# Causal mask of the attention scores added by VectorE in PSUM instead of by mask products on TensorE

## The chip, the core and the metric

The kernel runs on one NeuronCore of a Trainium2 chip (trn2). The core has TensorE for matrix products and transposes into PSUM, VectorE and ScalarE, which can read and write PSUM, GpSimd (POOL), which works on SBUF, and a queue for the DMAs on SyncE. Each engine runs its own instructions in the order in which they are written; between engines there are only semaphores. The metric is the device time of one launch in microseconds, lower is better.

## The reference

Two layers, each on 512 tokens of width 1024. In each, one normalised input goes through a combined projection to three groups of mixers: a gated delta rule (4 heads), native sparse attention (8 query heads of 64, 2 KV heads) and a short convolution. They are joined by an output projection, and a SwiGLU FFN follows. With 512 tokens there are 8 blocks of 64 and the 16 blocks that a query may choose take in all of them, and the window of 512 reaches back to the first token. So both the selected and the window branch are plain causal attention over all earlier tokens:

```
p_s = masked_softmax(jnp.einsum("bqgrd,bgqkd->bgrqk", q_r, k_g) * scale, smask)   # smask: kpos <= tq
p_w = masked_softmax(jnp.einsum("bqgrd,bkgd->bgrqk", q_r, kb) * scale, wmask)     # wmask: 0 <= dist < WINDOW
return gt[..., 0:1] * o_c + gt[..., 1:2] * o_s + gt[..., 2:3] * o_w
```

## The kernel before

The kernel writes the program of each engine as a function of the layer: `tensor_layer`, `scalar_layer`, `pool_layer`, `vector_layer`. The order of the work is written out by hand. Large products are done in three passes of fp32r (high x high, high x low, low x high), which is why weights and activations are split into a high and a low part.

A layer has three stages: the input projection with the work of the delta rule between its groups, the attention loop, and the output projection with the FFN. The change lies in the attention loop, which comes twice, once per layer.

The loop counts slots k from 0 to 23 (`N_SLOTS`), with some tail slots. `slot_of(k)` gives a pair of heads p (one of each KV head, a = 0 and 1), a branch br (selected or window) and a step s. Step 0 holds the query tiles 0 and 1, step 1 tile 2, step 2 tile 3 (`tiles_of`). The scores of one slot lie in two PSUM banks, one per a, and slots take turns between banks 0/1 and 2/3. For s = 0 tile 0 lies in columns 0 to 255 and tile 1 in 256 to 511; for s = 1 and 2 the tile has 384 or 512 columns. The causal mask matters only in the diagonal block of 128 columns of each tile, and in tile 0 for columns 128 to 255, which are computed only because products are 256 wide.

What each engine does in slot k, in its order:

- TensorE: `scores(k)`, which waits for the exponentials of slot k - 2 (line 1077), makes 6 products per tile (line 1083) and then adds the mask as products of a bf16 identity with the mask table `negm` (lines 1093, 1096). The last of them raises the semaphore `score`. Then come `p_transpose(k - 3)` (line 1109), which waits for GpSimd's scaling of those probabilities and for the copies of slot k - 4 out of banks 4 (VectorE) and 5 (ScalarE); every third slot the products with the values, `pv` (line 1126); in some slots the recurrence of the delta rule (`recur_first` line 1146, `recur_second` lines 1154 to 1161), the transposes of the compressed branch (line 1057) and of the delta rule's output (`gdn_out`, line 1170). In slots 11, 17 and 23 `cmp_pv` (line 1135) stands between the score products and the mask products.
- VectorE: `maximum(k)` (line 2349) reduces the masked scores to the negative row maximum and raises `nmax`; then `invert_sum(k - 1)` (line 2354), the copy `evacuate(k - 3)` (line 2360), and in some slots the softmax of the compressed branch (lines 2325 to 2337), the recurrence (lines 2369 to 2376), `mix_lo` (line 2401) and the root of the delta rule's norm (`gdn_finish`, lines 2384 to 2394). In slots 3, 5 and 14 the copy comes ahead of the maximum.
- ScalarE: `exp(k, 0)`, the copy `evacuate(k - 3)` (line 1450 in the profile, a helper's line), `exp(k, 1)` (line 1673; each exponential also reads its sum).
- GpSimd: `scale_probs(k)` (line 1917) after `inverse`, and from slot 18 on the pieces of the delta rule's output (lines 1925 and 1928), for which it waits on the last instruction of `gdn_finish`; `gdn_out` waits for these.

`chain(...)` on VectorE lets the engine wait until the instruction within has ended, so that the next can use its result. `negm` is 128 x 256 in bf16: columns 0 to 127 hold 0 on and below the diagonal and -1e30 above, the other 128 hold -1e30.

Of the kernel before, what the change touches and what calls it, by code (L numbers as in the profile page):

```python
# [12 lines left out]
ALU = mybir.AluOpType  # L13
ACT = mybir.ActivationFunctionType
AX = mybir.AxisListType.X

P = 128
# [71 lines left out]
def trunk(nc, A, out):  # L89
# [101 lines left out]
    with ExitStack() as ctx:  # L191
# [4 lines left out]
        S = Semaphores(nc, ctx)  # L196
# [3 lines left out]
        identb, negm = sb("identb", [P, P], BF16), sb("negm", [P, 2 * P], BF16)  # L200
# [18 lines left out]
        att = sb("att", [P, 2, 24])  # L219
        sb("spacer", [P, 10])  # L220
        x = sb("x_tok", [P, NT, D])
        hhi = sb("hT_hi", [P, KD, T], F32R)
# [311 lines left out]
        def tiles_of(s):  # L534

            return ((0, 1), (2,), (3,))[s]
# [157 lines left out]
        def tensor_layer(pe, l):  # L694
# [367 lines left out]
            def scores(k):  # L1062
                p, br, s = slot_of(k)
                b0 = bank_of(k)
                if k == 0:
                    pe.wait_ge(*S.at("klo", 1, l))
                    pe.wait_ge(*S.at("qlo", 1, l))
                    pe.wait_ge(*S.at("qnT", 3, l))
                elif k == 1:
                    pe.wait_ge(*S.at("ev_dve", 10, l))  # L1070
                    pe.wait_ge(*S.at("qlo", 2, l))
                elif k == 3:
                    pe.wait_ge(*S.at("klo", 2, l))
                elif k == 6:
                    pe.wait_ge(*S.at("qlo", 4, l))
                if k >= 2:
                    pe.wait_ge(*S.at("exp", exps_before(k - 1), l))
                for i in tiles_of(s):
                    n, c0 = max(256, (i + 1) * P), 256 if i == 1 else 0
                    for part in range(3):  # L1080
                        for a in range(2):
                            rows = slice(a * HEAD, (a + 1) * HEAD)
                            nc.tensor.matmul(ps[:, b0 + a, c0:c0 + n],  # L1083
                                             hhi[rows, (p, 4 + p, p)[part], i * P:(i + 1) * P],
                                             hlo[rows, (br, br, 2 + br)[part], 0:n],
                                             start=part == 0 and i != 1, stop=False, skip_group_check=True)
                if k % 6 == 5 and k >= 11:
                    cmp_pv((k - 11) // 6)
                for i in tiles_of(s):
                    c0 = 256 if i == 1 else 0  # L1090
                    for a in range(2):
                        if i == 0:
                            mm = nc.tensor.matmul(ps[:, b0 + a, 0:256], identb[:], negm[:], start=False, stop=True,
                                                  skip_group_check=True)
                        else:
                            mm = nc.tensor.matmul(ps[:, b0 + a, c0 + i * P:c0 + (i + 1) * P], identb[:], negm[:, 0:P],  # L1096
                                                  start=False, stop=True, skip_group_check=True)
                mm.then_inc(S["score"], 1)

            def p_transpose(k):  # L1100
                s = k % 3
# [864 lines left out]
        def vector_layer(dve, chain, l):  # L1966
# [375 lines left out]
            def maximum(k):  # L2342
                s, b0, col = k % 3, bank_of(k), att_at(k)
                dve.wait_ge(*S.at("score", k + 1, l))
                if s == 0:
                    v, n = ps[:, b0:b0 + 2, :].rearrange("p a (i c) -> p (a i) c", i=2), 4
                else:
                    v, n = ps[:, b0:b0 + 2, 0:(s + 2) * P], 2
                V.tensor_reduce(att[:, 0, col:col + n], v, AX, ALU.max, negate=True).then_inc(S["nmax"], 1)  # L2349

            def invert_sum(k):
                dve.wait_ge(*S.at("exp", exps_before(k + 1), l))
# [274 lines left out]
```

## Time and profile before

| | us |
|---|---|
| median of 3 runs | 1335.97 (1335.75 to 1336.1) |
| the profiled execution, its own time | 1336.82 |
| its span in the trace | 1335.1 |

| engine | busy us | instructions |
|---|---|---|
| TensorE, products | 1325.4 | 8936 |
| TensorE, weight loads | 1166.7 | 8936 |
| VectorE | 743.6 | 1434 |
| ScalarE | 625.0 | 1223 |
| GpSimd | 650.0 | 454 |

The granted TensorE clock is 1.000 over the span. In the page's chain of work that ended last TensorE has 95%. The times in a timeline are microseconds from the start of the span: start, duration, engine, line, operation, output and inputs with their shapes, and a count where instructions are merged. A bracket gives the idle time of the engine before the group and what ended it. "Idle" counts only gaps; a matmul's duration overlaps with that of the next, so the pace of TensorE is read from start to start.

### The profile page before, as it was taken

The numbers are of one execution on the slowest core, as the hardware profiler recorded it, in microseconds if no ns is written. First come the engines' busy times: TensorE is split into PE (matmuls) and PEld (weight loads), VectorE is DVE, ScalarE is ACT, GpSimd is POOL, SyncE is SP. The second block draws the span as 40 slices with busy tenths as digits, with TensorE's granted clock in tenths as the row PEclk, the third lists the DMA queues.
The fourth block names the chain that finished last, engine by engine and source line by source line (L and its number), as shares of the span: only waits on it lengthen the run. The fifth ranks groups of instructions, "written<-read, shape, count | busy, mean of one in ns | idle before, by whom it ended". The sixth has DMA issues, their size and how long they took to land.

```text
span 1335.1 us, 22359 instructions
## 1 busy us (share of the span) xinstructions
PE 1325.4 (99%) x8936; PEld 1166.7 (87%) x8936; DVE 743.6 (56%) x1434; ACT 625.0 (47%) x1223; POOL 650.0 (49%) x454
## 2 busy tenths in 40 slices
PE   8999999999999999999999999999999999999999
PEld 6888887778899889998879888887888998899987
DVE  5637777723876137771165387777248751477611
ACT  5563436636555225552335543467356542356511
POOL 4458307644454544554343663176435554354552
PEclk9999999999999999999999999999999999999999
DMA  7316300115333224333222352001233323334322
GB/s 169 127 37 161 96 17 1 33 41 94 95 96 116 98 88 114 108 96 118 87 84 79 75 157 77 1 2 33 64 96 92 98 95 111 95 96 120 103 88 86
DMA packets 176583, 114.91 MB, mean 86 GB/s; under 512 B 48224, under 2 KB 154976, under 8 KB 176480
## 3 DMA queue, kind: packets, MB, share of 16 engines
q1 hardware_dynamic: 174368, 113.22, 30.0%
q8 instruction: 71, 1.16, 0.4%
q10 hardware_dynamic: 2112, 0.26, 0.1%
q14 instruction: 32, 0.26, 0.1%
HBM read 109.80 MB, written 3.67 MB: 85 GB/s over the span
## 4 chain that ended last, share of the span: by engine, by line
PE 95%; DVE 2%; POOL 1%; issue 1%; DMA 1%; ACT 0%; SPq 0%; DVEq 0%
PE ps L796 35%; PE ps L1281 29%; PE ps L846 7%; PE ps L1182 7%; PE ps L1083 2%; PE ps L935 2%; PE ps L1126 2%; PE ps L1109 2%; PE ps L861 1%; PE ps L1135 1%; DMA x_tok<-in_x 1%; PE ps L915 1%; POOL arena L1917 1%; PE ps L1044 1%; PE ps L737 1%
## 5 line engine op out<-in xcount | busy, mean ns | idle before, releaser
L1820 POOL TENSOR_TENSOR w_lo<-w_raw,w_hi 128x2048 fp32r<-128x2048 f32 (+2 forms) x59 | 264.4, 4482 | 313.5 <-ACT w_hi L1386 245.4
L1386 ACT ACTIVATE w_hi<-w_raw 128x2048 fp32r<-128x2048 f32 (+2 forms) x61 | 113.9, 1866 | 232.5 <-PE ps L796 161.3
L1838 POOL TENSOR_TENSOR aT_lo<-ffn_tmp,aT_hi 128x512 fp32r<-128x512 f32 x44 | 63.5, 1443 | 167.4 <-ACT aT_hi L1433 167.4
L2564 DVE SCALAR_TENSOR_TENSOR x_tok<-ps,st,x_tok 128x512 f32<-128x512 f32 x32 | 23.8, 749 | 144.2 <-PE ps L796 144.2
L796 PE MATMUL ps<-w_hi,aT_hi 128*128 128x512 f32 x352 | 95.8, 390 | 0.0
L796 PE MATMUL ps<-w_lo,aT_hi 128*128 128x512 f32 x352 | 95.4, 389 | 0.0
L796 PE MATMUL ps<-w_hi,aT_lo 128*128 128x512 f32 x352 | 95.4, 389 | 0.0
L1394 ACT ACTIVATE w_hi<-w_raw 128x512 fp32r<-128x512 f32 x38 | 24.0, 632 | 131.9 <-PE ps L1281 96.1
L796 PE MATMUL ps<-hT_hi,w_lo 128*128 128x512 f32 x320 | 81.0, 393 | 0.0
L796 PEld LDWEIGHTS ps<-w_lo,aT_hi 128*128 128x128 f32 x352 | 66.1, 188 | 13.8
L796 PEld LDWEIGHTS ps<-w_hi,aT_lo 128*128 128x128 f32 x352 | 66.1, 188 | 13.8
L1281 PE MATMUL ps<-sT_hi,t_ring 128*128 128x256 f32 x480 | 77.2, 283 | 0.0
L796 PEld LDWEIGHTS ps<-w_hi,aT_hi 128*128 128x128 f32 x352 | 65.6, 188 | 13.2
L796 PE MATMUL ps<-hT_hi,w_hi 128*128 128x512 f32 x288 | 74.4, 398 | 0.0
L796 PE MATMUL ps<-hT_lo,w_hi 128*128 128x512 f32 x288 | 72.8, 392 | 0.0
L2477 DVE TENSOR_TENSOR ps<-w_raw 128x512 f32<-128x512 f32 x76 | 58.0, 764 | 24.0 <-DMA w_raw<-in_w_gate_up 24.0
L1832 POOL TENSOR_TENSOR w_lo<-w_raw,w_hi 128x512 fp32r<-128x512 f32 x38 | 49.2, 1294 | 44.9 <-ACT w_hi L1396 44.9
L796 PEld LDWEIGHTS ps<-hT_hi,w_lo 128*128 128x128 f32 x320 | 59.2, 188 | 11.7
L2505 DVE TENSOR_TENSOR ffn_tmp<-ps,rbt 128x256 f32<-128x256 f32 (+1 forms) x82 | 36.4, 443 | 58.8 <-PE ps L1281 58.3
L2349 DVE TENSOR_REDUCE att<-ps 128x4 f32<-128x1024 f32 (+2 forms) x48 | 54.3, 1131 | 22.9 <-PE ps L1096 22.5
L1450 ACT ACTIVATE arena<-ps 128x512 f32<-128x512 f32 (+4 forms) x80 | 41.7, 545 | 52.7 <-PE ps L970 26.4
L1281 PEld LDWEIGHTS ps<-sT_hi,t_ring 128*128 128x128 f32 x480 | 66.1, 190 | 0.0
(383 smaller groups left out, 3342.9 us busy)
## 6 DMA issues: line engine op xcount, KB each, us to landing
w_raw<-in_w_gate_up SPq DMA_DIRECT2D x88, 512.0 KB, 5.1
w_raw<-in_w_in SPq DMA_DIRECT2D x21, 1024.0 KB, 5.4
w_raw<-in_w_down SPq DMA_DIRECT2D x16, 1024.0 KB, 5.1
w_raw<-in_w_down SPq DMA_DIRECT2D x8, 768.0 KB, 4.4
w_raw<-in_w_out SPq DMA_DIRECT2D x16, 256.0 KB, 4.0
w_raw<-in_w_out SPq DMA_DIRECT2D x8, 512.0 KB, 5.0
w_raw<-in_w_in SPq DMA_DIRECT2D x2, 1056.0 KB, 7.2
x_tok<-in_x SPq DMA_DIRECT2D x4, 512.0 KB, 5.5
```

The costliest lines, as they stand in the source:

```text
L796: mm = nc.tensor.matmul(out_ap, a(ab, k), b(bb, k), start=first and i == 0, stop=last and i == len(kts) - 1)
L846: mm = nc.tensor.matmul(ps[:, in_bank(n, t), :], h[hp][:, half * KD // 2 + k, t * P:(t + 1) * P], W[wp][:, k, :], start=half == 0 and part ...
L1182: mm = nc.tensor.matmul(ps[:, OUT_BANKS[pair][t], :], mix[ab](OUT_KS[half][j])[:, t * P:(t + 1) * P], W[bb][:, j, :], start=first and part ...
L1281: mm = nc.tensor.matmul(out, w[:, k, :], h[:, k, :], start=first and part == 0 and k == 0, stop=last and part == 2 and k == 3, skip_group_ ...
L1386: nc.scalar.activation(whi[:, c % 2, 0:kt * w], raw[:, c % 2, 0:kt * w], ACT.Copy).then_inc(S["w_hi"], 1)
L1450: return nc.scalar.activation(dst, src, ACT.Copy, scale=scale)
L1820: nc.gpsimd.tensor_tensor(wlo[:, c % 2, 0:kt * w], raw[:, c % 2, 0:kt * w], whi[:, c % 2, 0:kt * w].bitcast(F32), ALU.subtract).then_inc(S ...
L1832: nc.gpsimd.tensor_tensor(dst[:, 4:6, :], src[:, 4:6, :], hi[:, 4:6, :].bitcast(F32), ALU.subtract)
L1838: nc.gpsimd.tensor_tensor(alo[:, cnt % FT, :], ft[:, cnt % 2, :], ahi[:, cnt % FT, :].bitcast(F32), ALU.subtract).then_inc(S["a_lo"], 1)
L2349: V.tensor_reduce(att[:, 0, col:col + n], v, AX, ALU.max, negate=True).then_inc(S["nmax"], 1)
L2477: V.tensor_tensor(t_bank(name), in0, in1, ALU.subtract).then_inc(S["sum"], 1)
L2505: V.tensor_tensor(dst, src, r, ALU.mult).then_inc(S["gsc"], 1)
```

## The change

`scores` no longer makes the mask products; the last score product raises `score`, ahead of `cmp_pv`. `maximum` adds the mask table to the diagonal blocks in PSUM first and waits for that. For s = 0 it does this with one addition over four blocks (columns 0 to 127 and 384 to 511 of both banks) and takes the maximum in two operations: tile 0 over its first 128 columns alone, tile 1 over 256. For s = 1 and 2 it is one addition over two blocks and one maximum.

```diff
@@ -1080,22 +1080,13 @@
-                            nc.tensor.matmul(ps[:, b0 + a, c0:c0 + n],
-                                             hhi[rows, (p, 4 + p, p)[part], i * P:(i + 1) * P],
-                                             hlo[rows, (br, br, 2 + br)[part], 0:n],
-                                             start=part == 0 and i != 1, stop=False, skip_group_check=True)
+                            mm = nc.tensor.matmul(ps[:, b0 + a, c0:c0 + n],
+                                                  hhi[rows, (p, 4 + p, p)[part], i * P:(i + 1) * P],
+                                                  hlo[rows, (br, br, 2 + br)[part], 0:n],
+                                                  start=part == 0 and i != 1, stop=part == 2, skip_group_check=True)
+                mm.then_inc(S["score"], 1)
                 if k % 6 == 5 and k >= 11:
                     cmp_pv((k - 11) // 6)
-                for i in tiles_of(s):
-                    c0 = 256 if i == 1 else 0
-                    for a in range(2):
-                        if i == 0:
-                            mm = nc.tensor.matmul(ps[:, b0 + a, 0:256], identb[:], negm[:], start=False, stop=True,
-                                                  skip_group_check=True)
-                        else:
-                            mm = nc.tensor.matmul(ps[:, b0 + a, c0 + i * P:c0 + (i + 1) * P], identb[:], negm[:, 0:P],
-                                                  start=False, stop=True, skip_group_check=True)
-                mm.then_inc(S["score"], 1)
@@ -2343,10 +2334,17 @@
                 if s == 0:
-                    v, n = ps[:, b0:b0 + 2, :].rearrange("p a (i c) -> p (a i) c", i=2), 4
+                    diag = ps[:, b0:b0 + 2, :].rearrange("p a (q c) -> p a q c", c=P)[:, :, 0:4:3, :]
+                    chain(V.tensor_tensor(diag, diag, negm[:, 0:P].rearrange("p (a q c) -> p a q c", a=1, q=1)
+                                          .broadcast_to([P, 2, 2, P]), ALU.add))
+                    first = att[:, 0, col:col + 4].rearrange("p (a i) -> p a i", i=2)
+                    V.tensor_reduce(first[:, :, 0], ps[:, b0:b0 + 2, 0:P], AX, ALU.max, negate=True)
+                    V.tensor_reduce(first[:, :, 1], ps[:, b0:b0 + 2, 2 * P:4 * P], AX, ALU.max, negate=True).then_inc(S["nmax"], 1)
                 else:
-                    v, n = ps[:, b0:b0 + 2, 0:(s + 2) * P], 2
-                V.tensor_reduce(att[:, 0, col:col + n], v, AX, ALU.max, negate=True).then_inc(S["nmax"], 1)
+                    diag = ps[:, b0:b0 + 2, (s + 1) * P:(s + 2) * P]
+                    chain(V.tensor_tensor(diag, diag, negm[:, 0:P].rearrange("p (a c) -> p a c", a=1).broadcast_to([P, 2, P]), ALU.add))
+                    V.tensor_reduce(att[:, 0, col:col + 2], ps[:, b0:b0 + 2, 0:(s + 2) * P], AX, ALU.max, negate=True
+                                    ).then_inc(S["nmax"], 1)
```

## Rows read from the trace of the kernel before

**Rows 1.** The page, busy time of each engine, its share of the span, instructions

```profile
PE 1325.4 (99%) x8936; PEld 1166.7 (87%) x8936; DVE 743.6 (56%) x1434; ACT 625.0 (47%) x1223; POOL 650.0 (49%) x454
```

**Rows 2.** Windows: length; busy PE, PEld, DVE, ACT, POOL; clock; DMA share; GB/s

```profile
195.80:216.80 21.00, 20.73 (x200) 17.09 (x200) 17.62 (x36) 12.88 (x43) 11.94 (x17) 1.00 0.01 2
216.80:242.00 25.20, 25.15 (x250) 20.79 (x248) 16.25 (x34) 15.20 (x50) 19.29 (x27) 1.00 0.03 8
242.00:258.30 16.30, 16.18 (x173) 12.30 (x173) 14.86 (x33) 12.11 (x38) 8.41 (x15) 1.00 0.18 56
258.30:267.90 9.60, 9.38 (x96) 6.97 (x96) 7.07 (x12) 5.93 (x21) 9.26 (x15) 1.00 0.01 3
...
856.00:928.10 72.10, 71.48 (x713) 57.19 (x713) 55.69 (x115) 46.13 (x149) 48.88 (x71) 1.00 0.06 16
```

**Rows 3.** Timeline of TensorE, slot 9 of layer 0 (s = 0)

```profile
222.71 0.39 PE L1093 MATMUL ps<-negm,identb 128*128 128x256 bf16 x2
222.94 0.28 PE L1096 MATMUL ps<-negm,identb 128*128 128x128 bf16 x2
223.14 1.03 PE L1109 MATMUL ps<-ident,arena 128*128 128x128 f32 x6
```

**Rows 4.** Timeline of TensorE, slot 8 of layer 0 (s = 2)

```profile
219.35 0.98 PE L1083 MATMUL ps<-hT_lo,hT_hi 64*128 64x512 f32 x6
220.26 0.28 PE L1096 MATMUL ps<-negm,identb 128*128 128x128 bf16 x2
220.38 1.04 PE L1109 MATMUL ps<-ident,arena 128*128 128x128 f32 x8
```

**Rows 5.** VectorE's groups by line and form: busy us, mean ns, idle before

```profile
L2349 DVE TENSOR_REDUCE att<-ps 128x2 f32<-128x1024 f32 x16 | 19.5, 1219 | 4.2 <-PE ps L1096 3.9
...
L2489 DVE TENSOR_TENSOR ps<-ps,w_raw 128x256 f32<-128x256 f32 x38 | 16.4, 432 | 16.4 <-ACT w_raw L1419 16.2
...
L2349 DVE TENSOR_REDUCE att<-ps 128x2 f32<-128x768 f32 x16 | 15.3, 956 | 17.3 <-PE ps L1096 17.3
```

**Rows 6.** Timeline of VectorE, a product in PSUM and the instruction that needs it

```profile
26.47 0.70 DVE L1971 TENSOR_TENSOR ps<-ps,rbt 128x512 f32<-128x512 f32 x1 [5.41 <-ACT rbt L1450]
27.20 0.75 DVE L1997 TENSOR_SCALAR arena<-ps,cw 128x512 f32<-128x512 f32 x1
```

**Rows 7.** Timeline of VectorE, slots 2 to 6: first and last of 23 groups

```profile
202.27 1.22 DVE L2349 TENSOR_REDUCE att<-ps 128x2 f32<-128x1024 f32 x1 [0.69 <-PE ps L1096]
...
216.14 0.41 DVE L2369 TENSOR_TENSOR arena<-arena,ps 128x256 f32<-128x256 f32 x1
```

**Rows 8.** Timeline of ScalarE, copies of slots 3 and 5 in slots 6 and 8

```profile
216.54 0.49 ACT L1450 ACTIVATE pbuf<-ps 128x384 f32<-128x384 f32 x1
...
222.92 0.59 ACT L1450 ACTIVATE spare<-ps 128x512 f32<-128x512 f32 x1
```

**Rows 9.** Timeline of TensorE, six transposes each in slots 6 and 7

```profile
212.05 0.83 PE L1109 MATMUL ps<-ident,pbuf 128*128 128x128 f32 x6
...
216.62 1.07 PE L1109 MATMUL ps<-ident,pbuf 128*128 128x128 f32 x6
```

**Rows 10.** Timeline of VectorE, slots 14 to 18

```profile
244.24 1.21 DVE L2349 TENSOR_REDUCE att<-ps 128x2 f32<-128x1024 f32 x1
...
246.96 0.17 DVE L2354 RECIPROCAL att<-att 128x2 f32<-128x2 f32 x1 [0.20 <-ACT spare L1673]
...
247.91 1.22 DVE L2384 TENSOR_REDUCE st<-arena 128x16 f32<-128x1024 f32 x1 [0.31 <-ACT arena L1718]
249.35 0.96 DVE L2349 TENSOR_REDUCE att<-ps 128x2 f32<-128x768 f32 x1 [0.22 <-PE ps L1096]
...
257.66 0.55 DVE L2394 SCALAR_TENSOR_TENSOR st<-st 128x16 f32<-128x16 f32 x1
```

**Rows 11.** The chain of work that ended last, in order of time, slots 18 to 22

```profile
258.29 0.62 POOL arena L1925
...
267.92 0.66 PE ps L1170 x4
```

## The prediction

> **What bounds the kernel now.** I began with the first part of the page, the busy share of each engine. TensorE is busy for 99% of the span and VectorE for 56% [rows 1]. Read alone, that says that work taken from TensorE is gained and work given to VectorE is free. A share over the whole span can't decide this, because the change touches only the attention loop, which runs once per layer for about 72 us. So I cut that loop of layer 0 into four stretches [rows 2]. In the first VectorE is busy 17.62 of 21.0 us, in the second 16.25 of 25.2, in the third 14.86 of 16.3, and in the fourth GpSimd is busy 9.26 of 9.6. TensorE's busy time is nearly full in all of them, but its matmuls are pipelined and overlap, so a wait of 0.1 or 0.2 us between two of them does not show. Layer 1 has the same loop 660.2 us later; its VectorE sum is 55.69 us [rows 2] against 55.80 for the four stretches of layer 0, so I work out layer 0 and double it. Then I read the timelines of VectorE and ScalarE slot by slot (a slot is one k, 24 per layer) to see who waits for whom.
>
> **What TensorE is spared.** In a slot with s = 1 or 2 two mask products go. They start at 220.26 and what follows them at 220.38, so they take 0.12 us of TensorE's issue [rows 4]. In a slot with s = 0 the two 256-wide ones take 222.71 to 222.94, 0.23 us, and the two narrow ones the same 0.12, together 0.35 [rows 3, 4]. Per layer: 8 x 0.35 + 16 x 0.12 = 4.7 us. The change of row groups ahead of the next full-height product stays. VectorE hears of the scores earlier too: the last score product ends at 219.35 + 0.98 = 220.33, the last mask product at 220.26 + 0.28 = 220.54, so 0.21 earlier [rows 4]. In slots 11, 17 and 23 the signal moves ahead of the compressed-branch product as well. That is worth something only where VectorE is already waiting.
>
> **What VectorE gets.** The trace holds the same sort of operation, an addition or product with PSUM both as input and output and one SBUF operand: 0.70 us for 512 elements [rows 6] and 432 ns for 256 [rows 5]. The 512-wide one is followed by a dependent instruction 0.73 us after its start (26.47 to 27.20), so the wait for its own result adds 0.03 us [rows 6]. The mask addition so costs 0.43 + 0.03 = 0.46 us for s = 1, 2 and 0.73 us for s = 0. No row here has a bf16 operand repeated over two blocks at this size; I bound the 256-wide addition by 0.40 and 0.56, the second if the strided blocks and the own wait cost 0.1 more, and take 0.46 because the 432 ns row is nearest in place and size. For s = 0 the one maximum over 1024 elements becomes two, over 256 and 512. The rows of 768 and 1024 elements, 956 and 1219 ns [rows 5], give 1.03 ns per element and 0.17 us fixed, so the two are 0.43 + 0.69 us; less the 0.08 us by which independent VectorE instructions overlap that is 1.04, 0.17 less than now (two sizes that no row has; 1.00 and 1.15 are the bounds). So a slot with s = 0 gains 0.73 - 0.17 = 0.56 us of VectorE and another 0.46. Per layer 8 x 0.56 + 16 x 0.46 = 11.8 us. With 4.7 us off TensorE, the exchange is a poor one wherever VectorE is on the path.
>
> The Trainium skill, "VectorE: DVE Perf Modes", section "The TRN2 errata", gives another price for a PSUM source, a fixed 120 cycles plus one per element at 0.96 GHz, so an estimate of 0.39 us for 256 elements. The rows' 0.43 is higher. By the page's price the forecast below would be some 0.8 us lower.
>
> **First stretch, slots 0 to 6.** The first idle time of VectorE that matters is the 0.69 us before the maximum of slot 2 at 202.27 [rows 7]. From there it works without a gap until its subtraction at 216.14 has ended. Until 202.27 TensorE has been spared the masks of slots 0 and 1 (0.35 + 0.12) and the signal of slot 2 comes 0.21 earlier, 0.68 in all, and just that idle time takes it up. From there on the additions of slots 2, 3, 4, 5 and 6 stand one behind another: 0.46 + 0.56 + 0.46 + 0.46 + 0.56 = 2.50 us. Net at slot 6: +1.8 us. Who waits for it: the exponentials of slot 6 start as soon as that maximum is done, and in ScalarE's queue the copy of the transposed probabilities of slot 3 at 216.54 lies behind them [rows 8]. TensorE's next transposes start at 216.62, and their second half needs that copy; this is why the six take 1.07 us where 0.83 is usual [rows 9]. So TensorE falls back by 1.8 us, and the masks it was spared in slots 3 to 7 only lengthen its wait.
>
> **Second stretch, slots 7 to 15.** VectorE has 9 us free of 25 [rows 2] and nearly all additions are hidden beside TensorE's products. One is not. In slot 8 the maximum stands right behind the state update, which itself waits for TensorE; the exponentials follow, then ScalarE's copy at 222.92, which ends at 223.51 [rows 8], and the second half of the transposes that start at 223.14 waits for it (1.03 us again) [rows 3]. That is +0.46, so +2.3. After it TensorE sets the pace and keeps what it is spared: slots 10 to 13 give 0.12 x 3 + 0.35 = 0.71, leaving +1.6 at slot 14.
>
> **Third stretch, slots 14 to 18.** The maximum of slot 14 (244.24) stands behind a state update that waits for TensorE [rows 10]. From here VectorE has only small gaps up to the end of 257.66 + 0.55 = 258.21: 0.20 within slot 15, 0.31 before 247.91 and 0.22 before 249.35 [rows 10]. The additions of slots 14 to 18 are 0.46 + 0.56 + 0.46 + 0.46 + 0.56 = 2.50; the three gaps and the lost overlaps take up about 0.9. Result: 1.6 + 2.5 - 0.9 = +3.2 us for the instruction that ends at 258.21.
>
> **Fourth stretch and after.** The instruction that ends at 258.21 is the last step of the roots for which GpSimd waits. Behind it GpSimd has a fixed chain that begins at 258.29, 9.26 of 9.6 us busy [rows 2], and TensorE's transposes at 267.92 wait for its end [rows 11]. What VectorE is late at 258.21 arrives in full. The masks of slots 18 to 22 are spared while TensorE waits anyway. After 267.92 TensorE is last again; slot 23 gives back 0.12, while slot 22's addition (0.46, less 0.21 of earlier signal) may delay the next output transposes by up to 0.2. I count this as nothing. So +3.2 us per layer, +6.4 for both. Against the profiled execution, whose own time is 1336.8 us, that is 1343.2; the median before is 0.85 us lower, 1335.97, so the prediction is 1342.4 us (+0.5%).
>
> **The rivals.** First, TensorE's relief counts in full. VectorE's 56%, the nearly full TensorE and 9 us of free VectorE time in the second stretch speak for it; then both layers gain 4.7 and the time is 1336.0 - 9.4 = 1326.6. Against it stand the gapless VectorE up to 216.55 and the exact meeting of 258.21 with 258.29. The Trainium skill, "Perfetto Trace Analysis", section "Identifying the Most-Contended Engine", says to optimise the engine of the highest occupancy first, which speaks for this rival; the same section warns that this engine can change over time. I give it 7%.
>
> Second, relief and additions cancel. At the five additions of the first stretch, one of the second and five of the third I count 5.5 us, against about 0.7 + 0.7 + 0.9 taken up. If an addition cost 0.25 us instead of 0.46 (work overlapped more than the rows show), 11 x 0.21 = 2.3 us per layer would go and 0.9 remain, 1337.8 in all; this is also what comes if the copies of slots 3 and 5 turn out not to hold TensorE. Within 0.2%: 11%.
>
> Third, every addition counts, since a later VectorE meets waits that are hidden now: 2 x (11.8 - 4.7) = 14.2, so 1350. The 9 us free in the second stretch speak against it. 8%. That the change would not do what it says, with the masks kept or added to the wrong blocks, I see no sign of in the diff: the added blocks are columns 0 to 127 and 384 to 511 for s = 0, and the half of tile 0's 256 columns that is no longer masked is not read by the new maximum.
>
> **How the numbers follow.** My own forecast has 74%. Its range: with the addition between 0.40 and 0.56 and about eleven on the path per layer, -1.3 to +2.2; if the relief of TensorE is 0.21 per slot instead of 0.12, as the ends of the instructions would have it [rows 4], another -1; if the waits of the second stretch and after 267.92 are 0.2 longer each, and the two maxima cost 1.15, another +1. That is 1340 to 1346. To leave out no more than two in ten, the range reaches down into the second rival, to 1337, and a little into the third, to 1347. A measurement of this kernel can tell about 0.2%, 2.7 us, from no change. Faster by more: 8%, the first rival and a little. Within: 12%. Slower by more: 80%.
>
> **What would show it.** In the changed profile the addition should read 0.42 to 0.45 us and 0.70 us, and VectorE's busy time should rise by some 23 us (24 busy less overlaps) while TensorE's instructions drop by 128. VectorE should have no idle time before the additions of slots 3 to 6 and 15 to 18; TensorE should wait in front of the second halves of the transposes in slots 7 and 9; the transposes behind GpSimd's chain should start near 271.1. If those start at 267.9 or earlier, the third stretch is read wrongly; if the first loop is ahead at slot 7, the first one is.

## The result, and the profile after

The changed kernel takes 1344.82 us (median of 4 runs, 1344.76 to 1345.05) against 1336.03 for the kernel before in the same session: a ratio of 1.0065, 95% interval 1.0053 to 1.0077, 8.8 us slower. The forecast was 1342.4 us with a range of 1337 to 1347, so sign and range held, and the size was 2.4 us short. The profiled execution of after has an own time of 1344.87 us and a span of 1343.1; before has 1336.82 and 1335.1, so these two differ by 8.05 us.

First the page of after, busy time of each engine and then the chain of work that ended last:

```profile
PE 1318.5 (98%) x8808; PEld 1159.6 (86%) x8808; DVE 763.3 (57%) x1498; ACT 625.2 (47%) x1223; POOL 651.3 (48%) x454
...
PE 88%; DVE 7%; issue 2%; ACT 1%; DMA 1%; POOL 1%; SPq 0%; DVEq 0%; ACTq 0%
```

TensorE has 128 instructions and 6.9 us less to do than in [rows 1], VectorE 64 instructions and 19.7 us more, and VectorE's part of the chain rose from 2% to 7%.

The new instructions, from VectorE's groups by line and form (busy us, mean ns, idle time before):

```profile
L2345 DVE TENSOR_TENSOR ps<-ps,negm 128x256 f32<-128x256 f32 x32 | 13.7, 428 | 12.1 <-PE ps L1083 11.6
L2338 DVE TENSOR_TENSOR ps<-ps,negm 128x512 f32<-128x512 f32 x16 | 11.1, 691 | 0.1
L2342 DVE TENSOR_REDUCE att<-ps 128x2 f32<-128x512 f32 x16 | 10.9, 680 | 0.0
...
L2341 DVE TENSOR_REDUCE att<-ps 128x2 f32<-128x256 f32 x16 | 6.8, 424 | 0.6
```

428 and 691 ns for the additions and 424 and 680 for the two maxima: each within 0.01 us of the price taken from the nearest rows.

The first three windows of [rows 2], moved with the work they hold (length; busy PE, PEld, DVE, ACT, POOL; clock; DMA share; GB/s):

```profile
195.20:218.08 22.88, 19.99 (x179) 15.94 (x179) 21.05 (x47) 12.90 (x43) 12.53 (x17) 1.00 0.00 1
218.08:243.23 25.15, 23.94 (x232) 19.82 (x231) 18.68 (x43) 14.85 (x50) 18.47 (x26) 1.00 0.03 3
243.23:261.15 17.92, 16.07 (x162) 12.00 (x162) 17.01 (x41) 12.47 (x39) 8.77 (x16) 1.00 0.22 60
```

The first and the third are longer by 1.88 and 1.62 us and VectorE fills 92 and 95% of them; the second, where it is busy 18.68 of 25.15 us, is as long as before. The granted clock is 1.00 in both kernels.

**Where the 8 us lie.** I measure the loop from the first transposes of its queries to the second transposes of its output. These two instructions of TensorE are, in before and then in after (layer 0, start and duration in us):

```profile
191.41 0.60 PE L1035 MATMUL ps<-ident,pbuf 128*128 128x128 f32 x4
...
271.27 0.60 PE L1170 MATMUL ps<-ident,arena 128*128 128x128 f32 x4
```

```profile
190.82 0.60 PE L1035 MATMUL ps<-ident,pbuf 128*128 128x128 f32 x4
...
270.94 0.60 PE L1161 MATMUL ps<-ident,arena 128*128 128x128 f32 x4
...
274.78 0.63 PE L1161 MATMUL ps<-ident,arena 128*128 128x128 f32 x4 [0.46 <-DVE aT_lo L2399]
```

The loop starts 0.59 us earlier in after (layer 0's first loads came earlier, and they don't depend on the edit) and reaches 271.27's counterpart 3.51 later: it grew by 4.10 us. In layer 1 the same sum is 4.19. The two make 8.3 us, between the 8.05 of the profiled executions and the 8.8 of the medians, so within 0.5 us the whole difference is the two loops. The shifts in the table are given against the start of the loop, with the 0.59 added.

| point in layer 0 | before | after | grown by | forecast |
|---|---|---|---|---|
| slot 6, VectorE's subtraction | 216.14 | 217.41 | 1.86 | 1.8 |
| slot 9, products behind its transposes | 224.10 | 225.85 | 2.34 | 2.3 |
| slot 14, copy of the state update | 242.07 | 243.31 | 1.83 | 1.6 |
| last step of the roots | 257.66 | 260.57 | 3.50 | 3.2 |
| first output transposes | 267.92 | 270.94 | 3.61 | 3.2 |
| second output transposes | 271.27 | 274.78 | 4.10 | 3.2 |

**First stretch.** VectorE's timeline of after in slots 2, 3 and 6 and then TensorE's in slots 7 and 9 (idle time before an instruction and its releaser in brackets):

```profile
201.09 0.43 DVE L2345 TENSOR_TENSOR ps<-ps,negm 128x256 f32<-128x256 f32 x1
...
204.51 0.69 DVE L2338 TENSOR_TENSOR ps<-ps,negm 128x512 f32<-128x512 f32 x1
205.24 0.42 DVE L2341 TENSOR_REDUCE att<-ps 128x2 f32<-128x256 f32 x1
205.58 0.68 DVE L2342 TENSOR_REDUCE att<-ps 128x2 f32<-128x512 f32 x1
...
217.41 0.41 DVE L2367 TENSOR_TENSOR arena<-arena,ps 128x256 f32<-128x256 f32 x1
```

```profile
217.65 0.52 PE L1100 MATMUL ps<-ident,pbuf 128*128 128x128 f32 x3 [1.14 <-DVE pbuf L2358]
218.45 0.52 PE L1100 MATMUL ps<-ident,pbuf 128*128 128x128 f32 x3 [0.28 <-ACT pbuf L1441]
...
224.76 1.16 PE L1100 MATMUL ps<-ident,arena 128*128 128x128 f32 x6 [0.80 <-DVE spare L2358]
```

Of the 0.69 us of idle time in front of slot 2 [rows 7] 0.14 is left (the instruction in front of 201.09 ends at 200.95), and from there no addition has idle time in front of it. A slot with s = 0 shows the steps: addition 0.69, 0.73 to the next start, two maxima 0.34 apart. At the end TensorE, which started its six transposes without any gap in [rows 9], waits 1.14 us for VectorE's copy and 0.28 for ScalarE's (0.49 us from 217.82, behind the exponentials). In slot 9 it waits 0.80 us, for VectorE's copy.

**Third stretch.** VectorE in slots 14 to 18, and then in slots 19 and 20:

```profile
243.31 0.42 DVE L2370 COPY arena<-ps 128x256 f32<-128x256 f32 x1 [0.58 <-PE ps L1152]
...
245.56 0.43 DVE L2345 TENSOR_TENSOR ps<-ps,negm 128x256 f32<-128x256 f32 x1
...
249.71 1.22 DVE L2382 TENSOR_REDUCE st<-arena 128x16 f32<-128x1024 f32 x1 [0.21 <-ACT arena L1709]
...
260.57 0.48 DVE L2392 SCALAR_TENSOR_TENSOR st<-st 128x16 f32<-128x16 f32 x1
260.97 0.42 DVE L2345 TENSOR_TENSOR ps<-ps,negm 128x256 f32<-128x256 f32 x1
...
263.60 0.42 DVE L2345 TENSOR_TENSOR ps<-ps,negm 128x256 f32<-128x256 f32 x1
...
265.27 0.67 DVE L2358 COPY spare<-ps 128x512 f32<-128x512 f32 x1
```

Of the three gaps of [rows 10] one is left, 0.21 us before 249.71, and the stretch grew by 1.67 us (forecast 1.6).

**Fourth stretch.** GpSimd's chain in after (its first and last operation before the output) and then TensorE:

```profile
261.13 0.61 POOL L1916 TENSOR_TENSOR arena<-arena,st 128x256 f32<-128x256 f32 x1
...
269.98 0.73 POOL L1919 TENSOR_TENSOR arena<-arena 128x256 f32<-128x256 f32 x1
```

```profile
266.09 1.16 PE L1100 MATMUL ps<-ident,arena 128*128 128x128 f32 x6 [0.94 <-DVE spare L2358]
...
270.23 0.87 PE L1100 MATMUL ps<-ident,arena 128*128 128x128 f32 x6
270.94 0.60 PE L1161 MATMUL ps<-ident,arena 128*128 128x128 f32 x4
```

VectorE of after, and then the lines of before that belong to the same slot, TensorE's scores and VectorE's maximum and subtraction:

```profile
270.34 0.43 DVE L2345 TENSOR_TENSOR ps<-ps,negm 128x256 f32<-128x256 f32 x1 [1.40 <-PE ps L1083]
270.81 0.96 DVE L2346 TENSOR_REDUCE att<-ps 128x2 f32<-128x768 f32 x1
...
273.94 0.69 DVE L2399 TENSOR_TENSOR aT_lo<-ps,aT_hi 128x512 fp32r<-128x512 f32 x1 [1.64 <-ACT aT_hi L1441]
```

```profile
266.19 0.79 PE L1083 MATMUL ps<-hT_lo,hT_hi 64*128 64x384 f32 x6
...
267.24 0.96 DVE L2349 TENSOR_REDUCE att<-ps 128x2 f32<-128x768 f32 x1 [2.27 <-PE ps L1096]
...
270.36 0.69 DVE L2401 TENSOR_TENSOR aT_lo<-ps,aT_hi 128x512 fp32r<-128x512 f32 x1 [1.64 <-ACT aT_hi L1450]
```

GpSimd ends at 270.71. The transposes at 270.94 stand right behind TensorE's own work and don't wait for it; TensorE is late because it waited 0.94 us at 266.09 for VectorE's copy of 265.27, which stands behind the additions of slots 19 and 20. The second pair (the transposes at 274.78) has its own path, here with shifts read straight from the two traces, without the 0.59: slot 22's scores start 3.32 us later than in before (269.51, 266.19), its maximum 3.57 later (270.81, 267.24), and behind it the exponentials and copies of ScalarE and VectorE's subtraction at 273.94 3.58 later (270.36 in before). TensorE, in before without a gap at 271.27, now waits 0.46 us for that subtraction.

### The profile page after: what moved, and what is told of

It reads as the page before. It is cut to its first block, busy times and chain, and to the rows that moved or that the text cites. A ratio compares the mean times of both kernels' runs of the same rounds, so it can differ in the third digit from the quotient of the medians.

```text
span 1343.1 us, 22167 instructions
## 1 busy us (share of the span) xinstructions
PE 1318.5 (98%) x8808; PEld 1159.6 (86%) x8808; DVE 763.3 (57%) x1498; ACT 625.2 (47%) x1223; POOL 651.3 (48%) x454
## 4 chain that ended last, share of the span: by engine, by line
PE 88%; DVE 7%; issue 2%; ACT 1%; DMA 1%; POOL 1%; SPq 0%; DVEq 0%; ACTq 0%
PE ps L796 33%; PE ps L1272 28%; PE ps L1173 7%; PE ps L846 6%; PE ps L935 2%; PE ps L1117 2%; PE ps L1100 1%; PE ps L1083 1%; DVE att L2346 1%; DVE ps L2345 1%; PE ps L1044 1%; PE ps L915 1%; PE ps L737 1%; PE ps L966 0%; DMA x_tok<-in_x 0%
## 5 line engine op out<-in xcount | busy, mean ns | idle before, releaser
L796 PEld LDWEIGHTS ps<-w_hi,aT_hi 128*128 128x128 f32 x352 | 65.6, 188 | 13.2
L796 PEld LDWEIGHTS ps<-hT_hi,w_lo 128*128 128x128 f32 x320 | 59.2, 188 | 11.8
L796 PEld LDWEIGHTS ps<-hT_lo,w_hi 128*128 128x128 f32 x288 | 53.5, 188 | 11.2 <-issue 0.3
```

The source lines that it names most:

```text
L796: mm = nc.tensor.matmul(out_ap, a(ab, k), b(bb, k), start=first and i == 0, stop=last and i == len(kts) - 1)
```

## The experiments

All times are medians, beside the kernel before on the same chip (1335.91 us for the first eight, 1335.88 for the last three). "Loop" is the growth of the stretch from the first query transposes to the second output transposes, layer 0 / layer 1, in the profiled execution.

| kernel | us | ratio, 95% | loop, us |
|---|---|---|---|
| the change | 1344.82 | 1.0065, 1.0053 to 1.0077 | +4.10 / +4.19 |
| e1, TensorE's side alone | 1332.02 | 0.9972, 0.9961 to 0.9982 | -2.24 / -2.17 |
| e2, VectorE's side alone | 1347.12 | 1.0083, 1.0069 to 1.0097 | +5.44 / +5.51 |
| e3, seven slots | 1334.50 | 0.9988, 0.9979 to 0.9997 | -0.93 / -0.84 |
| e4, two maxima alone | 1334.65 | 0.9991, 0.9982 to 1.0000 | -0.85 / -0.74 |
| e5, slots 2 to 6 undone | 1340.57 | 1.0035, 1.0021 to 1.0049 | +1.84 / +1.88 |
| e6, slots 14 to 18 undone | 1342.39 | 1.0048, 1.0034 to 1.0062 | +2.54 / +2.96 |
| e7, slots 19 to 23 undone | 1344.36 | 1.0063, 1.0049 to 1.0077 | +3.50 / +3.56 |
| e8, e3 and e4 together | 1333.33 | 0.9979, 0.9970 to 0.9989 | -1.53 / -1.43 |
| e9, masks ahead of `cmp_pv` | 1337.24 | 1.0010, 1.0001 to 1.0020 | +0.52 / +0.60 |
| e10, slot 8 alone | 1336.84 | 1.0006, 0.9997 to 1.0016 | +0.39 / +0.46 |
| e11, slot 10 alone | 1335.77 | 0.9998, 0.9989 to 1.0008 | -0.13 / -0.06 |

The sum of the two loops and the difference of the medians lie 0.1 to 0.5 us apart, in e5, e6 and e7 0.9 to 1.4. The loops come from one profiled execution of each kernel, and before's was itself 0.8 to 0.9 us over its median. Outside the loops, where the kernels are the same, the profiled executions are up to 1.0 us shorter and up to 0.2 us longer than before's. So small steps are judged by the loop; the intervals of e10 and e11 include 1, and their times alone show no change.

**e1: TensorE's side alone.** The kernel after without the two additions (two maxima kept), so it applies no mask at all:

```diff
-                    chain(V.tensor_tensor(diag, diag, negm[:, 0:P].rearrange("p (a q c) -> p a q c", a=1, q=1)
-                                          .broadcast_to([P, 2, 2, P]), ALU.add))
...
-                    chain(V.tensor_tensor(diag, diag, negm[:, 0:P].rearrange("p (a c) -> p a c", a=1).broadcast_to([P, 2, P]), ALU.add))
```

> The changed kernel without its additions: TensorE makes no mask products, the two maxima stay, and no mask is applied at all. It prices TensorE's side of the change (with the two maxima) alone. My theory (the loop hangs on VectorE's and GpSimd's queues in its first, third and fourth stretch, so only part of TensorE's relief arrives): per layer 0.7 us up to slot 2, 0.3 from the maxima of slots 3 and 6, 0.7 in slots 10 to 13, 0.3 from the maxima of slots 15 and 18, some 2.1 us; 1336.0 - 4.2 = 1331.8 us. Rival, TensorE is last everywhere: 2 x 4.7 us or more, 1326.6 us or below.

Measured 1332.02, the loops 2.24 and 2.17 us shorter. Of the 4.7 us that TensorE is spared per layer less than half arrives, although nothing was put on VectorE and the two maxima even relieve it. The first rival (1326.6) falls with this even before a single addition is paid.

**e2: VectorE's side alone.** `scores` as before, `maximum` as after, so the mask is added twice:

```diff
                 if s == 0:
-                    v, n = ps[:, b0:b0 + 2, :].rearrange("p a (i c) -> p (a i) c", i=2), 4
+                    diag = ps[:, b0:b0 + 2, :].rearrange("p a (q c) -> p a q c", c=P)[:, :, 0:4:3, :]
+                    chain(V.tensor_tensor(diag, diag, negm[:, 0:P].rearrange("p (a q c) -> p a q c", a=1, q=1)
+                                          .broadcast_to([P, 2, 2, P]), ALU.add))
...
```

> The kernel before with the changed maximum: TensorE still makes all mask products, and VectorE adds the mask a second time. It prices VectorE's side alone. My theory: slots 2 to 6 put 2.5 us on the path, slot 8 0.5, slots 14 to 18 2.5 less 0.9 of closed gaps, slots 19 to 22 another 0.5, so 5.1 us per layer and 1346.3 us. If the sides simply add up, 1344.8 plus what the tensor side alone gains (4.2 by my theory), 1349.0. If every addition counts (11.8 us per layer), 1359.6 us.

1347.12, 0.8 us over the expectation. 11.8 us more of VectorE per layer cost 5.5: over half is hidden, but what is left is more than e1's gain. The two loops sum to 5.44 - 2.24 = 3.20 where the change has 4.10, but e1 and e2 both hold the two maxima, and the sum counts these twice (so does the 1349.0 of the expectation). With e4 below, which has the two maxima and no addition, each side can be read twice, once with and once without the other:

- The additions cost 6.3 to 6.4 us per layer with no masks on TensorE (the change less e1) and 6.3 with them (e2 less e4), of 8 x 0.73 + 16 x 0.46 = 13.2 by their price.
- Taking the masks off TensorE brings 1.3 us with the additions there (e2 less the change) and 1.4 without (e4 less e1, where e4 has already halved tile 0's product), of 4.7.

So the sides add up to about 0.1 us. Each arrives only in part, TensorE's to less than a third.

**e3 and e4: only where TensorE sets the pace, and only the two maxima.** e3 moves the masks to VectorE in slots 0, 1 and 9 to 13, those in which the ledger has TensorE last; e4 leaves every mask on TensorE, makes two maxima for s = 0 and halves tile 0's mask product:

```diff
+VECTOR_MASK = (0, 1, 9, 10, 11, 12, 13)
...
+                if k in VECTOR_MASK:
+                    mm.then_inc(S["score"], 1)
...
+                if k in VECTOR_MASK:
+                    return
...
-                            mm = nc.tensor.matmul(ps[:, b0 + a, 0:256], identb[:], negm[:], start=False, stop=True,
+                            mm = nc.tensor.matmul(ps[:, b0 + a, 0:P], identb[:], negm[:, 0:P], start=False, stop=True,
```

In e4 the tuple is empty, and the last pair of lines isn't in e3.

> Mask by VectorE in slots 0, 1 and 9 to 13 only, where the trace of before shows VectorE with idle time ahead of the maximum and TensorE last; in all other slots the kernel before. My theory (it is the fullness of VectorE's queue that costs, not the longer way from score to exponential): relief of 0.47 us in slots 0 and 1 and 0.71 in slots 10 to 13 arrives, nothing is paid, 1.2 us per layer, 1333.7 us. Rival, the 0.25 us by which scores reach the exponentials later costs in each slot, wherever it is: seven slots x 0.25 x 2 = 3.5 us less the relief, 1336 to 1338 us.

> The kernel before, with the two maximum operations for tiles 0 and 1 alone, and tile 0's mask product therefore 128 columns wide instead of 256. Mask all by TensorE. The two maxima measure 0.42 + 0.68 us less an overlap of 0.08 against 1.22, so 0.2 us less of VectorE per slot with s = 0; TensorE is spared 0.11 in the same slots. My theory: slots 3, 6, 15 and 18 lie in the stretches where VectorE is last, 0.8 us, and TensorE's 0.1 in slots 0, 9 and 12 adds 0.2, so 1.0 us per layer, 1334.0 us. Rival, VectorE is not last there: only TensorE's 0.1 in eight slots, at best 1.7 us in all and in the places where VectorE matters nothing, 1335.5 us.

1334.50 and 1334.65, 0.8 and 0.65 us above their numbers and 1.4 and 1.3 below the kernel before; the loops are 0.7 to 0.9 shorter in both. e4's interval reaches up to 1.0000, so its gain rests on the loops. With the same edit in other slots the sign turns: what an addition costs is decided by its place, not by its 0.43 us.

**e5, e6, e7: one stretch each put back.** The kernel after with the slots of one stretch as in before:

```diff
+VECTOR_MASK = (0, 1, 7, 8, 9, 10, 11, 12, 13, 14, 15, 16, 17, 18, 19, 20, 21, 22, 23)
```

This is e5; in e6 the tuple lacks 14 to 18 instead, in e7 19 to 23.

> The changed kernel, with slots 2 to 6 undone (mask by TensorE and one maximum as before); the other 19 slots of a layer keep the change. My theory: at slot 6 TensorE stands at +1.87 us in the changed kernel and would stand at -0.47 with the relief of slots 0 and 1 alone; the difference of 2.3 us stays until the end, because each later stretch starts from where TensorE is. 1344.8 - 4.7 = 1340.1 us. Rival, a delay in the first stretch is taken up in the second, where VectorE has 9 us free: no more than 1 us, 1343.8 us or above.

> The changed kernel, with slots 14 to 18 undone. My theory: VectorE's stretch from the state update of slot 14 to the end of the roots in slot 18 then keeps the +1.8 us with which it starts instead of going to +3.45; the additions of slots 19 and 20 lose their place on the path as GpSimd's chain is then late less. 1.6 us per layer, 1344.8 - 3.2 = 1341.6 us. Rival, ScalarE's queue (exponentials of slot 15, the square ahead of them) sets that stretch: below 1 us in all, 1344 us.

> The changed kernel, with slots 19 to 23 undone. My prediction held the fourth stretch for GpSimd's fixed chain, whose beginning is set in slot 18, and counted slot 22's addition as nothing: then this kernel is as slow as the changed one or 0.2 us slower, 1344.8 to 1345.1 us. The trace of the changed kernel says otherwise: GpSimd's chain is +3.44 us late, the transposes behind it +3.6 and the second output transposes +4.1, with idle time until VectorE's low part. By that the additions of slots 19, 20 and 22 cost 0.65 us per layer: 1343.5 us.

The medians lie 0.5, 0.8 and 0.9 us over their expectations. e5 takes 2.3 us out of each loop: five additions cost the first stretch what the ledger says. e6 takes out 1.56 in layer 0, as expected, but 1.23 in layer 1. There VectorE's maximum of slot 17 starts late. First layer 1, then layer 0, in e6's timelines of TensorE (the mask products that release it) and VectorE:

```profile
916.40 0.29 PE L1102 MATMUL ps<-negm,identb 128*128 128x128 bf16 x2
...
252.90 0.29 PE L1102 MATMUL ps<-negm,identb 128*128 128x128 bf16 x2
```

```profile
917.15 1.23 DVE L2356 TENSOR_REDUCE att<-ps 128x2 f32<-128x1024 f32 x1 [0.50 <-PE ps L1102]
...
253.29 1.22 DVE L2356 TENSOR_REDUCE att<-ps 128x2 f32<-128x1024 f32 x1
```

It starts 0.46 us behind the end of the same pair in the one layer, 0.10 in the other. Why isn't known.

e7 tells the step that my forecast had wrong from the one that the trace of after shows. By the forecast the additions of slots 19 to 23 cost nothing, and the loop would stay at 4.1. It shrinks by 0.60 and 0.63 us. TensorE in e7:

```profile
270.80 0.66 PE L1176 MATMUL ps<-ident,arena 128*128 128x128 f32 x4 [0.25 <-POOL arena L1934]
...
274.14 0.60 PE L1176 MATMUL ps<-ident,arena 128*128 128x128 f32 x4
```

Now, as the forecast wanted it, GpSimd is last in front of the first pair, and the second pair has no wait. The median moved by only 0.46 us, less than twice 0.6, and the intervals of the two ratios overlap; so the reading of e7 rests on its loops and their waits.

**e8: the two edits that gained, together.** e3's slots and e4's two maxima.

> Both versions that were faster than the kernel before in one: mask by VectorE in slots 0, 1 and 9 to 13, by TensorE elsewhere, two maxima for tiles 0 and 1 with the 128-wide mask product. Gains of 1.4 and 1.3 us in different stretches should add up, 2.6 us, less 0.2 for slots 9 and 12, where both claim TensorE's time: 1333.4 us. If both gains come from the same place, 1334.4 us.

1333.33, as expected, and the fastest kernel here that applies the mask: 0.9979 (0.9970 to 0.9989) of the kernel before and 11.5 us under the change.

**e10, e11: one addition alone.** `VECTOR_MASK = (8,)`, said to be exposed, and `(10,)`, said to be hidden.

> The kernel before with the mask by VectorE in slot 8 alone (one slot per layer). My theory: there the maximum stands behind a state update that waits for TensorE, and TensorE's second half of transposes waits for what the exponentials let through; the addition of 0.46 us lies on the path and TensorE's relief of 0.12 only lengthens its wait. +0.4 to +0.5 us per layer within the loop. Rival, VectorE has 9 us free in this stretch, so one addition costs nothing: 0 or -0.1.

> The kernel before with the mask by VectorE in slot 10 alone, where VectorE has been idle for 3.07 us ahead of the maximum. The same edit as in slot 8, of the same size. My theory: TensorE is last, -0.12 us per layer within the loop. Rival, the longer way from score to exponential costs in any slot: +0.25 us per layer.

The loops grow by 0.39 and 0.46 and shrink by 0.13 and 0.06. The same instruction, the same 0.43 us: VectorE and then TensorE in e10, and VectorE in e11:

```profile
220.48 0.43 DVE L2367 TENSOR_TENSOR ps<-ps,negm 128x256 f32<-128x256 f32 x1
```

```profile
222.97 1.16 PE L1115 MATMUL ps<-ident,arena 128*128 128x128 f32 x6 [0.35 <-DVE spare L2380]
```

```profile
227.28 0.43 DVE L2367 TENSOR_TENSOR ps<-ps,negm 128x256 f32<-128x256 f32 x1 [2.86 <-PE ps L1084]
```

In slot 8 it stands right behind the state update, and TensorE waits for the copy behind it. In slot 10 VectorE had been idle for 2.86 us.

**e9: the earlier signal alone.** The kernel before with the mask products, and so the signal, ahead of the compressed branch's product in slots 11, 17 and 23:

```diff
-                if k % 6 == 5 and k >= 11:
-                    cmp_pv((k - 11) // 6)
                 for i in tiles_of(s):
...
                 mm.then_inc(S["score"], 1)
+                if k % 6 == 5 and k >= 11:
+                    cmp_pv((k - 11) // 6)
```

> The kernel before with one thing moved: in slots 11, 17 and 23 the mask products, and with them the signal that the scores are ready, come ahead of the compressed branch's product, so VectorE hears 0.86 us earlier. That is a part of the change, alone. My theory: in slot 11 VectorE's wait is hidden, in slot 17 VectorE is busy until 0.04 us before its maximum, in slot 23 it comes from other work too; 0.0 us per layer, 1335.9 us. Rival, the earlier signal is worth something in slot 17, at the head of a full stretch: up to 0.1 us for each of the layers.

Both theories missed: it is slower, 1337.24, each loop 0.5 to 0.6 longer. In layer 0 the first output transposes stand 0.19 us further back than in before and the second, with slot 23 between them, 0.52. TensorE in slot 11, before and then e9:

```profile
229.87 1.02 PE L1135 MATMUL ps<-arena,vcr 64*128 64x512 f32 x2
230.82 0.29 PE L1096 MATMUL ps<-negm,identb 128*128 128x128 bf16 x2
230.94 0.50 PE L1109 MATMUL ps<-ident,spare 128*128 128x128 f32 x3
```

```profile
229.74 0.29 PE L1094 MATMUL ps<-negm,identb 128*128 128x128 bf16 x2
229.96 1.12 PE L1135 MATMUL ps<-arena,vcr 64*128 64x512 f32 x2
231.01 0.76 PE L1109 MATMUL ps<-ident,spare 128*128 128x128 f32 x5
```

The scores and `cmp_pv` use 64 rows of the array, masks and transposes all 128. In before there is one change between 64 and 128 rows here, in e9 there are three; changes between bf16 and f32 operands are two in both. The scores start 0.22 us earlier than in before (228.85, 229.07), the transposes 0.07 later, so the slot takes 0.29 us more of TensorE. That the changes of rows are what costs is my reading of these lines; no kernel has such a change alone. The change itself has no mask products and doesn't pay this; e9 therefore doesn't measure what its signal is worth. That it is worth nothing in slot 17 is read from after: the addition at 253.93 has no idle time before it.

## Why the prediction was right, and where it fell short

**VectorE is the bound of two stretches, at 56% of the span: held.** e1, e2 and e5 show both sides of the exchange, e10 and e11 one addition in either place. The Trainium skill, "Perfetto Trace Analysis", section "Identifying the Most-Contended Engine", has the engine of highest occupancy treated first, and judges TensorE not by the busy share of its products but by MFU (its share of peak arithmetic) and the busy share of its weight loads. By either busy share that engine is TensorE here (99% and 87%, VectorE 56%), and taking work off it at VectorE's cost lost 0.65%. That this engine can change over time, which the prediction places in the same section, stands in the next one, "Optimization Strategy", and it is what decided.

**Prices of the new instructions: held.** Additions 0.428 and 0.691 us, 0.46 and 0.73 to the next start. The price by the Trainium skill, "VectorE: DVE Perf Modes", section "The TRN2 errata", 0.39 us for 256 elements, was too low by 0.04. It is worked out from the section's row for PSUM to SBUF. For an fp32 `tensor_tensor` addition the same section has 151 cycles plus one per element, an estimate of 0.42 and 0.69 us, and the trace agrees with it. The two maxima end 1.02 us after their start (205.24 to 206.26), taken as 1.04.

**VectorE busy +23 us: read 19.7.** From the groups of after the additions are 24.8 us (13.7 + 11.1) and the two maxima 1.8 less than the one (17.7 against 19.5), 23.0 together. Two maxima overlap by 0.08, 1.3 us for sixteen pairs; the other 2 us are overlap as well: VectorE's instructions added up one by one come to 792.1 us in before and 815.3 in after, 23.2 more, and what they overlap grew by 3.5. No time hangs on it.

**First stretch +1.8: held, 1.86.** Of the relief of 0.68 the addition of slot 2 could use 0.59 (201.09 + 0.59 against 202.27), and from its start to 217.41 the five additions took 2.45 (forecast 2.50). The path to TensorE was the one named and one more: it waits first for VectorE's own copy (1.14 us), and ScalarE's adds 0.28.

**Second stretch: the sign of each slot held, the relief was over-counted.** Slot 8 brings the growth to 2.34 (forecast 2.3; e10 0.39 and 0.46), but the wait in slot 9 is for VectorE's copy, not for ScalarE's alone. From there to slot 14 the relief is 0.51 instead of 0.71. The term that was too large is the 0.12 us for a slot with s = 1 or 2. TensorE in after, and the instruction that follows in before:

```profile
220.63 0.97 PE L1083 MATMUL ps<-hT_lo,hT_hi 64*128 64x512 f32 x6
221.53 1.09 PE L1100 MATMUL ps<-ident,arena 128*128 128x128 f32 x8
222.46 0.60 PE L1057 MATMUL ps<-ident,arena 128*128 128x128 f32 x4
```

```profile
221.27 0.60 PE L1057 MATMUL ps<-ident,arena 128*128 128x128 f32 x4
```

From the scores to the next transposes behind the eight: 219.35 to 221.27 [rows 4], 1.92 us; in after 1.83. The relief is 0.09, not 0.12: the eight transposes take 0.04 to 0.05 longer when they follow the 64-row products themselves, which I read as a part of the change of rows that the mask products had borne. Other slots show 0.06 to 0.09, and a slot with s = 0 gives 0.29 instead of 0.35. e11 says the same: by the copy of the state update in slot 14, TensorE's only relief being slot 10's, its two layers are 0.07 and 0.06 us ahead. Of the 0.13 by which its layer 0 ends shorter the other half arises behind that. By this 0.2 us are missing in each layer from slot 14 on, of the 0.9 that were missing in all.

**Third stretch +1.6: held, 1.67.** e6 takes it out in layer 0; layer 1 is 0.3 to 0.4 off, not explained.

**Fourth stretch +0: this is the step that failed; it is +0.6.** I wrote that what VectorE is late at 258.21 arrives in full through GpSimd's fixed chain, that the masks of slots 18 to 22 are spared while TensorE waits anyway (the additions of slots 19 to 21 stand in no term), and that slot 22's addition "may delay the next output transposes by up to 0.2. I count this as nothing". The first half held only in the sum: GpSimd starts 3.43 later (258.29 to 261.13) and ends 3.43 later, but it is no longer last. TensorE is, held at 266.09 by VectorE's copy behind the additions of slots 19 and 20, and comes to 3.61. The second half was wrong. What I had set against each other, slot 22's addition and its earlier signal, is right as a difference (shifts without the 0.59 again): 3.57 less 3.32 is 0.25, and 0.46 less 0.21 is 0.25. But its scores start 3.32 later where the first output transposes come only 3.02 later, since TensorE's own queue was held at 266.09 and in before those transposes had been waiting for GpSimd, which slot 22's path had not. So this path has fallen 3.58 - 3.02 = 0.56 us behind the first pair. In before 0.22 us lay between its end and the transposes, 271.27 - (270.36 + 0.69); in after, where they wait for it, 274.78 - (273.94 + 0.69) = 0.15 still do. So only 0.07 was slack, and 0.49 comes on top of the 0.11 by which the first pair stands later than in e7 (3.61, 3.50). I had looked at the addition alone and neither at the start nor at the slack of the path that it is on. e7 shows the whole term: 0.60 and 0.63 us per layer. How it divides between the additions of slots 19, 20 and 22 is read from the trace and wasn't tried one by one.

**The sum.** 3.2 forecast per layer; 0.2 to 0.3 of it too little before the roots (mostly the relief), 0.6 after them: 4.1. Twice that is 8.3 instead of 6.4. The rest of the 2.4 us by which the median was missed, 0.5, is what separates the medians from the loops of the profiled pair.

**The rivals.** Relief in full: e1 and e2 exclude it. Cancelling: the additions cost 0.46, not 0.25, and TensorE did wait for the copies. Every addition counts (1350): excluded by e2 (5.5 of 11.8 us) and by e11; but the fourth stretch went its way: by the trace three additions that had no term there, of slots 19, 20 and 22, weren't hidden.

## What to carry to other kernels

Before work is moved from a full engine to one that is half idle, cut the loop into stretches and ask in each whose queue is full: an addition of 0.43 us cost 0.4 us where work stood right in front of it and a consumer right behind it, and gained 0.1 where the engine had been idle for 2.86 us, and moving it only in such slots turned +0.65% into -0.12% (-0.21% with the two maxima). When a chain on a third engine is last, compute the slack of every other chain that ends at the same consumer, and take off the time that lies between release and start even where the consumer waits: of 0.22 us that looked free 0.07 was. Two runs that share a part of the edit can't be summed before that part is taken out once. Of a removed instruction count what its follower takes over from it: here a quarter to a half of the 0.12 us.

## What the runs showed of the hardware

- With one more change back and forth between products on 64 and on 128 rows of TensorE's array, slot 11 of e9 took 0.29 us more, over twice what the two mask products take (0.12). The order of the products is all that differs.
- Eight transposes on 128 rows took 1.09 us right behind 64-row products in after, 1.04 behind mask products in before.
- GpSimd's operations of 256 elements in the fourth stretch take 0.60 to 0.74 us, but single ones 1.19 (262.63 in before) or 1.06 (266.16 in after), at other places in each kernel; the chain as a whole grew by nothing. The cause wasn't tried.
- In one of the two layers of e6 VectorE started slot 17's maximum 0.46 us after the end of the products that released it, in the other 0.10; in before such starts come 0.04 us after it (267.24 behind 267.20). This stays open.
